# Folding a short routing tile and scoring cached keys on VectorE and POOL in a hybrid decoder step

## Chip, cores and metric

One Trainium2 chip, one of its cores. The metric is the device time of one execution in microseconds. The kernel before takes 4506.3 us, median of three runs (4504.82 to 4509.7).

## What is computed

One layer of a model with two kinds of heads and a retrieval of experts, for 512 prompt tokens (with 16 learned tokens ahead) and for 8 samples of 4 new tokens, whose past is cached: 256 keys each, in two pages of 128, found through a page table. Everything is float32. Cut to what matters here:

```python
# 8 gated-delta heads ("gdn") and 8 softmax heads with a forget gate ("fox"), head width 128
fq_s, fk_s, fv_s, logf_s = fox_inputs(qkv_fs, f_fs, ...)           # samples: 32 queries in all
k_past = cache_k[l][page_table].reshape(8, 256, FOX_HEADS, HEAD_DIM)
s = einsum('bqhd,bkhd->bhqk', q, k) * HEAD_DIM ** -0.5 + cq - ck   # each sample against its own 256 keys
p = softmax(where(kpos <= qpos, s, -inf))                         # over past and new keys
# experts: per token 8 heads, top 16 of 128 x 128 product keys, then
y = sum over 16 * 8 experts of gate * gelu(x . expert_u[idx]) * expert_v[idx]
```

## The kernel before, in words

**Groups.** 560 tokens are cut in two groups. FIRST has 256 columns (two tiles of 128; the first 32 are the samples' new tokens). LATER has 304 (tiles of 128, 128 and 48 rows). `front` (L245) runs for each: norm and gates, `heads` (L589), `mix_out`, `ffn_norm`, `route` (L2154). While LATER is worked on, a stream of expert rows runs beside it, and `rest_of_experts` finishes it.

**Heads.** In one loop of 8 heads come the projections (64 segments of 16 matmuls, L861), a gdn head and a fox head, half a head apart. Each engine has an in-order list, and it is written out by hand: every step is yielded with a mark, and `Marks` (L545) merges the lists of `gdn`, `fox`, `projections` and the like by it. 100 marks are one head; `fox_mark(h)` (L580) is 100 h + 50, called `at`. A late result therefore holds up all that stands behind it on its engine.

**The samples' cached scores.** `cached` (L767) loads 16 pages of keys and of values a head, keys on partitions. `sampled` (L1022) turns the keys on PE (L1033, 16 transposes, marks at+9 and at+12.5) into two PSUM banks; ACT (L1300) and VectorE, called DVE (L1567), copy them back. At at+17 PE adds the forget sums (L1045 to L1049) and the products of keys and queries (L1051): one 128x128 weight load for 4 columns, 16 times. DVE copies the scores (L1571), PE turns them (L1062), then softmax (L1574, L1304), turning (L1067, L1068) and values (L1076), and L1082. The prompt's own attention (L1129 to L1152) begins at mark at+`START`, which is 40, in steps of `EACH`, 24.

**What stands beside it.** At these marks gdn inverts a matrix in six levels: PE's L952 and L958 and DVE's L1479, L1483 and L1487 in turn. Then PE's L976, DVE's vN (L1500), PE's L985, ACT's copy, DVE's um (L1505) and POOL's ub (L1658), PE's L991. On SP: keys and values to scratch (L817, L822), weight loads (L747), cached pages (L776). On ACT's queue each weight segment is stored to scratch (L1199). POOL stores keys and values (L1676).

**Stream.** Each of 1088 items is an indirect load of 128 rows of 8 KB by POOL (L1854) into a ring of six, and one pass of DVE (L1932 with u, L1943 or L1947 with v). 448 items come from FIRST's routing; the rest are known when LATER's routing is done. `OVERLAP` (L306) says how many items each stage takes in: 14, 330, 48, 8 and 48, in all 448. `Share` spreads them over a stage's steps. `spread` (L1824) moves the indices of split tiles.

**Routing.** Per head PE projects queries (L2224), ACT copies them (L2245), PE scores each tile (L2232), ACT copies (L2254), DVE finds the best 16 twice: MAX8 (L2291), FIND_INDEX8 (L2294), MATCH_REPLACE8 (L2298), one each per tile and half, first on the scores, then on 80 candidates; then one-hot products over all tiles (L2342, L2345, L2347).

Of the kernel before, what the change touches and what calls it, by code (L numbers as in the profile page):

```python
# [29 lines left out]
P = 128  # L30
D = 2048
KT = D // P
# [29 lines left out]
class Group:  # L62
# [7 lines left out]

    def __init__(self, tag, base, edges, slot):
# [6 lines left out]
        self.own = slice(slot, slot + self.n)  # L78

# [111 lines left out]
def build(nc, ins, outs):  # L191
    with ExitStack() as ctx:
# [5 lines left out]
        def cst(name, a=0, b=None):  # L198
# [11 lines left out]
            "kT": nc.dram_tensor("kT_scratch", (HEADS, P, KA), F32, kind="Internal").ap(),  # L210
            "v": nc.dram_tensor("v_scratch", (HEADS, KA, HD), F32, kind="Internal").ap(),
# [94 lines left out]
OVERLAP = {"norm": 14, "heads": 330, "out": 48, "ffn": 8, "route": 48}  # L306
# [282 lines left out]
def heads(nc, ins, outs, mem, scr, group, stream, quota):  # L589
# [12 lines left out]
    PAGE_SETS = 4  # L602
# [17 lines left out]
        + ("past_turned past_even past_odd columns_ready past_scores scores_copied new_scores "  # L620
# [19 lines left out]
                "kc": ([P, PAGES, HD],), "vc": ([P, PAGES, HD],),  # L640
# [25 lines left out]
    START, EACH = (40.0, 48.0 / T) if samples else (22.0, 64.0 / T)  # L666
# [39 lines left out]
    def blocks_of(t):  # L706

        return blocks[:group.slot + t + 1]

# [23 lines left out]
    with ctx:  # L733
# [3 lines left out]
        def _(sp):  # L737
# [28 lines left out]
            def cached():  # L766
# [3 lines left out]
                for h in range(HEADS):  # L770
                    for own, buffer, used, step in (("k", B.kc, "past_scores", 36.0), ("v", B.vc, "s_out", 44.0)):
# [32 lines left out]
            def fox():  # L804
                yield -90.0
                sp.wait_ge(sem["f_cleared"], 5)
                for h in range(HEADS):
# [5 lines left out]
                    if samples:  # L813
# [6 lines left out]
                        for j in range(T):  # L820
                            a, b = blocks[j]
                            sp.dma_start(scr["v"][h, a:b, :], values_of(j)).then_inc(sem["v_kept"], 16)  # L822
                    else:
# [23 lines left out]
        def _(pe):  # L847
# [172 lines left out]
            def sampled(h, at):  # L1020
                n, q0 = h + 1, B.f_qkvT[:, h % 2, 0, :]
                yield at + 9  # L1022
                for i in range(PAGE_SETS):
                    if i == 2:
                        yield at + 12.5
                    if i == 0:
                        pe.wait_ge(sem["k_past"], n * 16 * PAGES)
                    if i < 2:
                        pe.wait_ge(sem[("f_k_copied", "f_v_copied")[i]], n)
                    else:  # L1030
                        pe.wait_ge(sem[("past_even", "past_odd")[i % 2]], h * 2 + 1)
                    for j in range(4):
                        last = nc.tensor.transpose((B.F1, B.F2)[i % 2][:, j * P:(j + 1) * P], B.kc[:, 4 * i + j, :], ident)  # L1033
                    last.then_inc(sem["past_turned"], 1)

# [1384 lines left out]
```

## Time and profile before

| | |
|---|---|
| median of three runs | 4506.3 us (4504.82 to 4509.7) |
| the profiled execution | 4511.9 us, its span 4510.2 us |
| mean granted TensorE clock | 0.753 |
| busy: PE, DVE, ACT, POOL | 53%, 74%, 13%, 52% |
| DMA | 1513.71 MB, mean 336 GB/s |

PE is TensorE's matmul part, PEld its weight loads. The shares are means over stages with different limits, so they say little: heads of FIRST run to about 890 us, LATER's front from about 1250 to 2867, the rest of the stream to the end. Times in the rows are us from the span's start; PEclk is the granted TensorE clock as a share of 2.4 GHz.

### The profile page before, as it was taken

Reading aid. Unit: us, or ns where it says so; the run is one execution under the profiler, and the core shown is the slowest. Engines: PE = TensorE matmul, PEld = TensorE weight load, DVE = VectorE, ACT = ScalarE, POOL = GpSimd, SP = SyncE. Lnnn points to the kernel's source line nnn. Section 1 sums busy time; section 2 is a strip of 40 time slices with the busy share of each in tenths; the row PEclk is TensorE's granted clock in tenths of the full one; section 3 lists DMA queues with packets and bytes.
Section 4 is the critical chain, followed back from the end, with each engine's and each line's share of the span. In section 5 each row is a group of like instructions: output and inputs, shape, how many; then the busy total and the mean of one; then the engine's idle time right before and its main releaser. Section 6 shows DMA issues by size and latency. Waiting matters only on the chain. (4 is left out here: it accounts for less than half of the span.)

```text
span 4510.2 us, 35350 instructions
## 1 busy us (share of the span) xinstructions
PE 2386.0 (53%) x11713; PEld 1883.7 (42%) x11713; DVE 3326.5 (74%) x4469; ACT 589.8 (13%) x1450; POOL 2331.3 (52%) x1217
## 2 busy tenths in 40 slices
PE   6999999898488888888849755100000000000000
PEld 5888888787466666656537544000000000000000
DVE  2333332306779999989876789899998989999997
ACT  1222222201122222222210011000000000000000
POOL 1010010000246666555665322588888888888886
PEclk8999999899699999999969877555555555555555
DMA  6766666487779999999999865699999999999998
GB/s 177 223 206 201 192 197 202 143 299 245 282 283 400 396 391 417 409 368 398 372 389 413 342 243 202 262 422 422 420 420 407 422 413 420 422 415 419 412 410 350
DMA packets 443935, 1513.71 MB, mean 336 GB/s; under 512 B 42045, under 2 KB 276209, under 8 KB 277849
## 3 DMA queue, kind: packets, MB, share of 16 engines
q0 software_dynamic: 161840, 1158.85, 63.4%
q1 hardware_dynamic: 269240, 251.94, 17.5%
q10 hardware_dynamic: 12672, 100.67, 5.6%
q8 instruction: 93, 1.52, 0.1%
q14 instruction: 90, 0.73, 0.0%
HBM read 1384.96 MB, written 126.21 MB: 335 GB/s over the span
## 5 line engine op out<-in xcount | busy, mean ns | idle before, releaser
L1932 DVE CUSTOM_DVE_ANT_0 ex_ring<-ex_ring,ex_xi 128x2048 f32<-128x2048 f32 x544 | 1244.5, 2289 | 125.4 <-DMA ex_ring<-in_peer_u_dram,ex_idx_s 45.6
L1947 DVE SCALAR_TENSOR_TENSOR ex_y<-ex_ring,ex_wt,ex_y 128x2048 f32<-128x2048 f32 x538 | 1264.4, 2350 | 96.9 <-DMA ex_ring<-in_peer_v_dram,idx_all 52.9
L1854 POOL DMA_INDIRECT ex_ring<-in_peer_v_dram,idx_all x384 | 809.2, 2107 | 252.5 <-DVE ex_y L1947 135.6
L1854 POOL DMA_INDIRECT ex_ring<-in_peer_u_dram,idx_all x384 | 786.5, 2048 | 285.1 <-DVE ex_hid L1932 175.1
L861 PE MATMUL heads_b_pj<-xnT_b,lead 128*128 128x304 f32 x2048 | 600.5, 431 | 6.9 <-PEq L283 3.6
L1886 PE MATMUL ex_fold<-ex_y,const 128*32 128x512 f32 (+1 forms) x48 | 26.9, 727 | 1090.5 <-DVE ex_y L1947 1041.3
L1886 PEld LDWEIGHTS ex_fold<-ex_y,const 128*32 128x32 f32 (+1 forms) x48 | 6.7, 143 | 1110.2 <-DVE ex_y L1947 1042.2
L1854 POOL DMA_INDIRECT ex_ring<-in_peer_v_dram,ex_idx_s x160 | 304.0, 1900 | 273.9 <-DVE ex_y L1947 192.9
L861 PEld LDWEIGHTS heads_b_pj<-xnT_b,lead 128*128 128x128 f32 x2048 | 375.4, 196 | 117.3 <-issue 14.7
L1854 POOL DMA_INDIRECT ex_ring<-in_peer_u_dram,ex_idx_s x160 | 320.2, 2001 | 190.5 <-DVE ex_hid L1932 144.8
L861 PE MATMUL heads_a_pj<-xnT_a,heads_a_w 128*128 128x256 f32 x1216 | 315.9, 397 | 1.8 <-DMA heads_a_w<-in_w_in_dram 1.8
L861 PEld LDWEIGHTS heads_a_pj<-xnT_a,heads_a_w 128*128 128x128 f32 x1216 | 226.6, 199 | 32.5 <-issue 2.9
L1904 ACT ACTIVATE ex_act<-ex_hid 128x16 f32<-128x16 f32 x34 | 7.3, 216 | 1731.0 <-DVE ex_hid L1932 1731.0
L861 PE MATMUL heads_a_pj<-xnT_a,lead 128*128 128x256 f32 x832 | 214.2, 397 | 3.5 <-PEq L281 3.5
L1850 POOL DMA_DIRECT2D ex_xi<-xi_scratch x13 | 7.0, 550 | 355.6 <-POOLq L281 300.5
L861 PEld LDWEIGHTS heads_a_pj<-xnT_a,lead 128*128 128x128 f32 x832 | 156.0, 199 | 24.7 <-issue 5.8
L2030 PE MATMUL out_b_acc<-out_b_w,mixT_b 128*128 128x256 f32 (+1 forms) x672 | 147.5, 380 | 3.3 <-DMA out_b_w<-w_out_scratch 2.6
L2030 PEld LDWEIGHTS out_b_acc<-out_b_w,mixT_b 128*128 128x128 f32 (+1 forms) x672 | 111.5, 168 | 39.3 <-issue 4.4
L1676 POOL DMA_DIRECT2D out_k_prompt_dram<-heads_a_f_kN x16 | 8.9, 561 | 220.8 <-ACT heads_a_f_kN L1295 220.8
L1658 POOL TENSOR_TENSOR heads_a_ub<-heads_a_uN,const 128x1024 f32<-128x1024 f32 x8 | 15.7, 1966 | 192.8 <-ACT heads_a_uN L1252 192.8
L2030 PE MATMUL out_a_acc<-out_a_w,mixT_a 128*128 128x256 f32 x448 | 100.5, 388 | 6.0 <-DMA out_a_w<-in_w_out_dram 6.0
L1664 POOL DMA_DIRECT2D out_gdn_sample_dram<-heads_a_sout x8 | 7.6, 952 | 181.1 <-DVE heads_a_sout L1524 181.1
(582 smaller groups left out, 4012.0 us busy)
## 6 DMA issues: line engine op xcount, KB each, us to landing
lead<-w_scratch SPq DMA_DIRECT2D x64, 1024.0 KB
heads_a_w<-in_w_in_dram SPq DMA_DIRECT2D x38, 1024.0 KB, 6.1
w_scratch<-heads_a_w ACTq DMA_DIRECT2D x38, 1024.0 KB, 4.1
lead<-in_w_in_dram SPq DMA_DIRECT2D x26, 1024.0 KB, 5.8
w_scratch<-lead ACTq DMA_DIRECT2D x26, 1024.0 KB, 4.2
out_a_w<-in_w_out_dram SPq DMA_DIRECT2D x7, 2048.0 KB, 14.0
w_out_scratch<-out_a_w ACTq DMA_DIRECT2D x7, 2048.0 KB, 7.7
out_b_w<-w_out_scratch SPq DMA_DIRECT2D x7, 2048.0 KB, 12.7
```

The source lines that it names most:

```text
L861: last = nc.tensor.matmul(pj[j % PJ][:, 0:N], slot(j)[:, k, :], xnT[:, k, :], start=(k == 0), stop=(k == KT - 1))
L1658: nc.gpsimd.tensor_tensor(B.ub[:], B.uN[:, 0, :].unsqueeze(1).to_broadcast([P, NB, HD]), cst("members", 0, NB).unsqueeze(2).to_broadcast([ ...
L1664: pool.dma_start(outs["gdn_sample"][0, :, h].rearrange("b k v -> k b v"), B.sout[:]).then_inc(sem["gs_out"], 16)
L1676: pool.dma_start(out[place, h, :], rows[own_rows, t, :]).then_inc(sem[f"{own}_out{t}"], 16)
L1850: pool.dma_start(self.tokens(s)[part.on, :], self.xi_rows[part.xi_rows]).then_inc(self.sem["xi_in"], 16)
L1854: pool.indirect_dma_start(self.ring[:, i % RING, :], None, self.tables[which], bass.IndirectOffsetOnAxis(ap=self.index(s, g, k), axis=0)). ...
L1886: last = self.nc.tensor.matmul(self.fold[0:rows, c:c + BANK], self.mem["cst"]("ident", r * rows, (r + 1) * rows), self.sum_of(s)[:, c:c + ...
L1904: self.nc.scalar.activation(self.act[:, g % 2, :], self.hid[:, g % 2, :], ACT.Gelu).then_inc(self.sem["activated"], 1)
L1932: nc.vector.tensor_tensor_reduce(ring, ring, self.tokens(s)[:], 1.0, 0.0, ALU.mult, ALU.add, self.hid[:, g % 2, k:k + 1]).then_inc(self.se ...
L1947: nc.vector.scalar_tensor_tensor(y, ring, wt, y, ALU.mult, ALU.add).then_inc(self.sem["consumed"], 1)
L2030: last = nc.tensor.matmul(acc[0:b - a, i, 0:GW], mixT[:, k, a:b], weights[:, k, :], start=(k == 0), stop=(k == KT - 1))
```

## The change

Two parts. **Routing of LATER** is folded: `folded` is true where the last tile has at most 64 rows (48 here). ACT puts the 48 query columns of an even head in the first, of an odd head in the second half of `q_fold`; even heads route two tiles, odd heads two and one of 96 rows, which holds both heads. `spread` takes the indices from there (two transfers in place of one for such a part). `OVERLAP` for routing falls from 48 to 36, so that 12 known items are left for the end.

**The cached scores** are formed from unturned keys. PE turns the 32 queries as well (behind L1104), ACT copies them to `q_row`, SP stores them to scratch (16 KB) and loads them back to all 128 partitions (`q_all`, 2 MB). For each of 8 samples a product of 2 pages x 4 queries x 128 is formed, 4 on POOL and 4 on DVE, and DVE reduces all 8 over the width. It adds the sums to PE's forget sums. Later steps of `sampled` move back by 12 marks, START and EACH become 52 and 19.

The diff below goes through OVERLAP and the helpers, then SP (cached pages, then `fox`), PE (`sampled`, then `fox`), ACT, DVE, POOL and routing.

```diff
-OVERLAP = {"norm": 14, "heads": 330, "out": 48, "ffn": 8, "route": 48}
+OVERLAP = {"norm": 14, "heads": 330, "out": 48, "ffn": 8, "route": 36}
-    START, EACH = (40.0, 48.0 / T) if samples else (22.0, 64.0 / T)
+    START, EACH = (52.0, 38.0 / T) if samples else (22.0, 64.0 / T)
+    SPLIT = NB // 2
+    def products(b):
+        shape = [P, 2, NQ, HD]
+        return (B.kc[:, 2 * b:2 * b + 2, :].unsqueeze(2).to_broadcast(shape),
+                B.q_all[:, NQ * b:NQ * (b + 1), :].unsqueeze(1).to_broadcast(shape))
...
-                                sp.wait_ge(sem[used], h)
+                                    sp.wait_ge(sem["pool_products"], SPLIT * h)
+                                    sp.wait_ge(sem["vector_products"], (NB - SPLIT) * h)
...
+                        yield at + 9.5
+                        sp.wait_ge(sem["q_rows"], n)
+                        sp.dma_start(scr["q"][h].rearrange("(q d) -> q d", d=HD), B.q_row[:]).then_inc(sem["q_kept"], 16)
+                        yield at + 12
+                        sp.wait_ge(sem["q_kept"], 16 * n)
+                        sp.dma_start(B.q_all[:].rearrange("p q d -> p (q d)"), scr["q"][h].partition_broadcast(P)
+                                     ).then_inc(sem["q_wide"], 16)
...
-                    for b in range(NB):
-                        last = nc.tensor.matmul(B.F1[:, page * NS + NQ * b:page * NS + NQ * (b + 1)], B.kc[:, 2 * b + page, :],
-                                                q0[:, NQ * b:NQ * (b + 1)], start=False, stop=(b == NB - 1))
-                yield at + 20.5
+                yield at + 32.5
-                yield at + 26
+                yield at + 38
-                yield at + 30
+                yield at + 42
-                yield at + 35
+                yield at + 47
...
+                        pe.wait_ge(sem["f_q_normed"], n)
+                        last = nc.tensor.transpose(B.F1[0:NS, 3 * P:3 * P + HD], qkv[:, 0, 0:NS], ident)
...
-                            nc.scalar.copy(B.kc[:, 4 * i:4 * i + 4, :].rearrange("p n c -> p (n c)"), B.F1[:]
-                                           ).then_inc(sem["past_even"], 1)
+                        nc.scalar.copy(B.q_row[:], B.F1[0:NS, 3 * P:3 * P + HD]).then_inc(sem["q_rows"], 1)
...
+                        for i in range(SPLIT):
+                            b = NB - SPLIT + i
+                            yield at + 16 + 3.5 * i
+                            if i == 0:
+                                dve.wait_ge(sem["q_wide"], 16 * n)
+                                dve.wait_ge(sem["k_past"], n * 16 * PAGES)
+                            nc.vector.tensor_tensor(B.product[:, 2], *products(i), ALU.mult).then_inc(sem["vector_products"], 1)
+                            yield at + 17 + 3.5 * i
+                            nc.vector.tensor_reduce(B.sK[:, :, NQ * i:NQ * (i + 1)], B.product[:, 2], AX_X, ALU.add
+                                                    ).then_inc(sem["summed"], 1)
+                            yield at + 19 + 3.5 * i
+                            dve.wait_ge(sem["pool_products"], SPLIT * h + i + 1)
+                            nc.vector.tensor_reduce(B.sK[:, :, NQ * b:NQ * (b + 1)], B.product[:, i % 2], AX_X, ALU.add
+                                                    ).then_inc(sem["summed"], 1)
+                        yield at + 31
+                        nc.vector.tensor_tensor(B.sT[:], B.F1[:, 0:2 * NS], B.sK[:].rearrange("p n q -> p (n q)"), ALU.add
+                                                ).then_inc(sem["scores_copied"], 1)
...
+                    for i in range(SPLIT):
+                        yield at + 16 + 3.5 * i
+                        if i == 0:
+                            pool.wait_ge(sem["q_wide"], 16 * n)
+                            pool.wait_ge(sem["k_past"], n * 16 * PAGES)
+                        if SPLIT * h + i >= 2:
+                            pool.wait_ge(sem["summed"], 2 * (SPLIT * h + i - 1))
+                        nc.gpsimd.tensor_tensor(B.product[:, i % 2], *products(NB - SPLIT + i), ALU.mult
+                                                ).then_inc(sem["pool_products"], 1)
...
+    def tiles_of(h):
+        rows = list(group.rows)
+        if folded:
+            rows = rows[:-1] + ([2 * fold_rows] if h % 2 else [])
+        return rows
...
+                    if folded:
+                        nc.scalar.copy(B.q[:, s, 0:fold_at], pq[s][:, 0:fold_at])
+                        place = slice(h % 2 * fold_rows, (h % 2 + 1) * fold_rows)
+                        last = nc.scalar.copy(B.q_fold[:, s, place], pq[s][:, fold_at:N])
```

ACT's and DVE's marks of the samples' softmax move back by 12 like PE's. In routing every operation of ACT and DVE goes over `tiles_of(h)` and the first T tiles of its buffers.

## Rows read from the trace of the kernel before

**Rows 1.** Stretches: PE, PEld, DVE, ACT, POOL busy; PEclk; DMA share; GB/s
```profile
128.90:841.10 712.20, 697.23 (x3978) 607.17 (x3978) 227.77 (x688) 190.56 (x463) 69.73 (x77) 0.95 0.64 198
2708.70:2744.60 35.90, 21.33 (x76) 15.19 (x76) 32.83 (x99) 3.43 (x20) 9.91 (x6) 0.79 0.64 233
2880.00:4480.00 1600.00, 16.66 (x32) 4.31 (x30) 1470.32 (x973) 9.30 (x23) 1372.78 (x643) 0.51 1.01 417
```

**Rows 2.** One line, L1104: ns least/median/most, first and last start
```profile
L1104 PE MATMUL heads_a_F<-const,heads_a_f_qkvT x16: 272/273/273, 129.1 to 841.2; 128*128 128x128 f32 x16
```

**Rows 3.** Groups by shape, DVE, one route head (2708.7 to 2744.6)
```profile
L2291 DVE MAX8 route_b_top<-route_b_sc 128x8 f32<-128x128 f32 x8 | 1.7, 280 | 0.1
...
L2342 DVE TENSOR_TENSOR route_b_hot<-route_b_place,const 128x816 f32<-128x816 f32 x1 | 1.0, 1008 | 0.0
...
L2342 DVE TENSOR_TENSOR route_b_hot<-route_b_place,const 128x768 f32<-128x768 f32 x1 | 1.0, 959 | 0.0
...
L2291 DVE MAX8 route_b_top<-route_b_sc 48x8 f32<-48x128 f32 x4 | 0.9, 268 | 0.0
```

**Rows 4.** Timeline, DVE, the same head (start, us, what)
```profile
2725.89 1.24 DVE L2291 MAX8 route_b_top<-route_b_sc 128x8 f32<-128x128 f32 x6
...
2727.35 0.28 DVE L2294 FIND_INDEX8 route_b_at<-route_b_top,route_b_sc 128x8 uint32<-128x128 f32 x1
...
2727.61 0.29 DVE L2294 FIND_INDEX8 route_b_at<-route_b_top,route_b_sc 128x8 uint32<-128x128 f32 x1
```

**Rows 5.** Timeline, seam of routing and rest, and DVE's last items
```profile
2862.57 4.82 DVE L1947 SCALAR_TENSOR_TENSOR ex_y<-ex_ring,ex_wt,ex_y 128x2048 f32<-128x2048 f32 x2 [0.58 <-DVEq L170]
...
2866.59 1.67 POOL L1854 DMA_INDIRECT ex_ring<-in_peer_u_dram,idx_all  x1 [0.30 <-issue]
...
2875.16 2.29 DVE L1932 CUSTOM_DVE_ANT_0 ex_ring<-ex_ring,ex_xi 128x2048 f32<-128x2048 f32 x1 [7.77 <-DMA ex_ring<-in_peer_u_dram,idx_all]
...
4488.30 4.81 DVE L1947 SCALAR_TENSOR_TENSOR ex_y<-ex_ring,ex_wt,ex_y 128x2048 f32<-128x2048 f32 x2
```

**Rows 6.** Groups by shape, PE, heads of the first group (128.9 to 841.1)
```profile
L1051 PE MATMUL heads_a_F<-heads_a_f_qkvT,heads_a_kc 128*128 128x4 f32 x224 | 33.6, 282 | 0.0
...
L1033 PE MATMUL heads_a_F<-const,heads_a_kc 128*128 128x128 f32 x112 | 14.5, 273 | 0.0
```

**Rows 7.** Stretches of 4 us behind L1051 (columns as rows 1)
```profile
446.00:450.00 4.00, 4.00 (x33) 3.98 (x32) 0.00 (x0) 0.00 (x0) 0.00 (x0) 0.86 0.77 229
450.00:454.00 4.00, 4.00 (x15) 3.23 (x15) 0.23 (x1) 0.00 (x0) 0.00 (x0) 0.50 0.00 0
```

**Rows 8.** Timeline, PE, head 3 (start, us, what)
```profile
434.98 0.38 PE L1104 MATMUL heads_a_F<-const,heads_a_f_qkvT 128*128 128x128 f32 x2
...
450.44 3.78 PE L861 MATMUL heads_a_pj<-xnT_a,heads_a_w 128*128 128x256 f32 x8
454.01 1.06 PE L952 MATMUL heads_a_R<-heads_a_yX,heads_a_EN 128*128 128x128 f32 x4
...
464.08 0.38 PE L985 MATMUL heads_a_R<-heads_a_vN,heads_a_yX 128*128 128x128 f32 x2
```

**Rows 9.** DMA landings of L822 (v_scratch), then of w_out_scratch
```profile
DMA to landing us min/median/max: 1.6/3.4/6.4
...
DMA to landing us min/median/max: 6.2/7.7/12.2
```

**Rows 10.** One line each: ns least/median/most, first and last start
```profile
L1524 DVE TENSOR_TENSOR heads_a_sout<-heads_a_sout,heads_a_R x8: 1220/1222/1222, 182.6 to 880.2; 128x1024 f32<-128x1024 f32 x8
...
L1644 POOL TENSOR_TENSOR heads_a_sout<-heads_a_state,heads_a_tails x8: 1887/1997/2032, 90.7 to 801.9; 128x1024 f32<-128x1024 f32 x8
...
L1505 DVE TENSOR_SCALAR heads_a_um<-heads_a_uN,const x8: 285/288/2024, 158.9 to 863.4; 128x128 f32<-128x128 f32 x8
```

**Rows 11.** Timeline, last head: PE and POOL
```profile
862.58 0.30 PEld L985 LDWEIGHTS heads_a_R<-heads_a_vN,heads_a_yX 128*128 128x128 f32 x2 [0.92 <-DVE heads_a_vN L1500]
...
863.46 1.89 POOL L1658 TENSOR_TENSOR heads_a_ub<-heads_a_uN,const 128x1024 f32<-128x1024 f32 x1 [17.73 <-ACT heads_a_uN L1252]
```

More of the change, by code:

```diff
@@ L78, in __init__ @@
         self.own = slice(slot, slot + self.n)
+        self.folded = self.n > 1 and 2 * self.rows[-1] <= P
     def prompt_rows(self, i):
@@ L770, in cached @@
                 for h in range(HEADS):
-                    for own, buffer, used, step in (("k", B.kc, "past_scores", 36.0), ("v", B.vc, "s_out", 44.0)):
+                    for own, buffer, step in (("k", B.kc, 36.0), ("v", B.vc, 46.0)):
                         for i in range(PAGES):
@@ L1021, in sampled @@
                 n, q0 = h + 1, B.f_qkvT[:, h % 2, 0, :]
[L1022 to L1034, printed above, removed]
                 yield at + 17
-                pe.wait_ge(sem["past_even"], 2 * n)
-                pe.wait_ge(sem["past_odd"], 2 * n)
+                pe.wait_ge(sem["f_k_copied"], n)
+                pe.wait_ge(sem["f_v_copied"], n)
+                pe.wait_ge(sem["q_rows"], n)
                 pe.wait_ge(sem["columns_ready"], n)
@@ L1700, in __init__ @@
             self.on = slice(p, p + rows.stop - rows.start)
+            self.folded = group.rows[tile] if group.folded and tile == group.n - 1 else 0
             first = group.base + group.tiles[tile][0]
@@ L1827, in spread @@
                 for table, source in ((self.idx_s, self.mem["idx_all"]), (self.gate_s, self.mem["gate_all"])):
-                    sp.dma_start(table[part.on, s.at:s.at + s.groups * TOPK],
-                                 source[part.rows, part.slot, part.head:part.head + s.groups, :].rearrange("p h k -> p (h k)")
-                                 ).then_inc(self.sem["spread"], 16)
+                    place = table[part.on, s.at:s.at + s.groups * TOPK]
+                    if part.folded:
+                        place = place.rearrange("p (h e k) -> p h e k", e=2, k=TOPK)
+                        for e in range(2):
+                            rows = slice(part.rows.start + e * part.folded, part.rows.stop + e * part.folded)
+                            sp.dma_start(place[:, :, e, :], source[rows, part.slot, part.head + 1:part.head + s.groups:2, :]
+                                         ).then_inc(self.sem["spread"], 16)
+                    else:
+                        sp.dma_start(place, source[part.rows, part.slot, part.head:part.head + s.groups, :]
+                                     .rearrange("p h k -> p (h k)")).then_inc(self.sem["spread"], 16)
     def spread_all(self, group):
-        return sum(32 * len(s.parts) for s in self.sets if not s.whole and (s.group is FIRST or s.group is group))
+        return sum(64 if part.folded else 32 for s in self.sets if not s.whole and (s.group is FIRST or s.group is group)
+                   for part in s.parts)
     def gather(self, pool, taken):
@@ L2252, in _ @@
                         act.wait_ge(sem["scores_read"], h)
[L2253 removed]
+                    for i, r in enumerate(tiles_of(h)):
                         last = nc.scalar.copy(B.sc[0:r, i, s, :], ps[s][0:r, i * KEYS:(i + 1) * KEYS])
@@ L2302, in _ @@
                 order = Counter(dve, sem["dve_order"], h, 100)
+                rows = [slice(0, r) for r in tiles_of(h)]
+                T = len(rows)
+                own = slice(group.slot, group.slot + T)
                 share.take(dve, h * PARTS + 1)
@@ L2305, in _ @@
                     dve.wait_ge(sem[f"scores_copied{s}"], h + 1)
-                rows = [slice(0, r) for r in group.rows]
                 top16(order, [(B.sc[rows[t], t, s, :], B.top[rows[t], t, s, :], B.at[rows[t], t, s, :])
```

113 lines of the change are left out of this document (61 added, 52 removed).

## Prediction

> **What bounds the kernel now.** I read the table of stretches first, then groups, timelines and landings. Three stretches matter. In the first group's heads (L1104 starts once a head, from 129.1 to 841.2: seven periods of 101.7 us [rows 2]) PE is busy 697.2 of 712.2 us, DVE 32% and DMA 0.64: PE sets the time, and sits idle only 2 us a head [rows 1]. Routing of the later group (one head period, 2708.7 to 2744.6) has DVE busy 32.8 of 35.9 us with DMA at 0.64: DVE sets it. From 2880 on DMA stands at 1.01: the expert stream is bound by transfers [rows 1]. So a change pays in heads if it leaves PE less to do without making PE wait; in routing if it shortens DVE.
>
> **Folded routing.** Even heads of the later group drop the 48-row tile; odd heads take it for both, 96 rows in one, and an instruction's time does not depend on its rows: MAX8 takes 268 ns on 48 rows and 280 on 128 [rows 3]. In the timeline six MAX8 take 1.24 us (0.21 each) and finds follow at 0.26 to 0.27 [rows 4], as I take for replaces. A tile dropped is 2 x (2 x 0.21 + 2 x 0.27 + 0.27) = 2.4 us on scores, about 1.0 on candidates (the 80-wide forms), and a third of six instructions over 816 and 768 elements, (1008 - 959) / 48 = 1.02 ns an element: 3 x (0.28 + 0.26) = 1.6; smaller ones 0.3. That is 5.3 us, and four even heads make **-21.2 us**. DVE hides nothing of it. ACT's and PE's chain to the next scores runs under DVE's items and table work, and keeps cover with 1.1 items a step in place of 1.5; if not, DVE waits, which is a rival below.
>
> Twelve stream items move behind routing: 12 x 2.42 us off DVE (L1947, 2.35 and a gap) = -29.0, and back at the stream's pace. That pace is (4493.1 - 2875.2) / 640 items = 2.53 us [rows 5]: +30.3. But the seam changes. Now all 448 known items are used up in routing; the first gather with new indices is issued at 2866.6 and DVE sits until 2875.2, 7.8 us [rows 5]. Afterwards six landed items wait in the ring. DVE's last route item ends at 2867.3 - 21.2 - 29.0 = 2817.1; a barrier, 1 us by choice; the next gather follows its first item (2.4) and lands 8.6 later (the same 2866.6 to 2875.2): 2829.1; then 646 items x 2.528 = 1633.1, end 4462.2 against 4493.1. **Folding in all: -31 us**, bounds -24 (the seam gives nothing) and -33. The four more small index transfers are needed hundreds of us later: nothing.
>
> **Cached scores, what PE loses.** 16 transposes a head go (L1033, 14.5 us in seven heads, 1.76 in place, where neighbours overlap), and 32 passes of four columns (L1051, 33.6 / 7 = 4.8 us) [rows 6]. Behind L1051 the granted clock falls, to 0.86 and then 0.50, which is the 1.2 GHz level [rows 7], and the eight L861 at 450.4 take 3.57 us to the next row [rows 8], in place of 1.73 where the clock is full. From L1104 (434.98) to L985 (464.08), 29.1 us [rows 8], PE would be done in 19.6: removed 1.76 + 4.45, clock 1.84 + 0.8, L1062, L1067 and L1068 moved behind (1.2), one added transpose and its wait (0.5). Alone this would be -8.4 us a head.
>
> **What it gets instead** is a chain from L1104 to L985. ACT copies keys, then queries: 1.1 us. SP is behind its two L822 issues: q write issued at +1.5. Landing: least / median / most of L822's v_scratch stores are 1.6 / 3.4 / 6.4 us [rows 9]; I take 3.4, since it stands in the same queue. The broadcast (2 MB into 128 partitions) has no row; the nearest with its bytes and 16 KB runs is w_out_scratch, 6.2 / 7.7 / 12.2 [rows 9]; I take 7.7, the median, as other transfers run beside both. So queries are wide at **+12.7 us**, bounds +9.4 and +15 (a quarter of both slow sides). Estimate from the Trainium skill (DMA: Bandwidth & Descriptors, Bandwidth and the anatomy of one DMA), which gives about 436 GB/s and 2 us fixed: 6.8 us, by which the sum would end 7 us lower; no row here shows a broadcast undisturbed.
>
> From there DVE, in order: before the vN that L985 waits for stand four multiplies and seven reductions of 1024 elements. L1524 of that size takes 1.22 us [rows 10], 1.25 with the gap to the next: 13.8 us. Four of gdn's own (0.42) and vN (0.34) make 15.8. POOL's products (L1644's shape, 2.0 us) read two SBUF operands meanwhile, and DVE's L1505, 0.29 us by its median, took up to 2.02, beside POOL's L1658 [rows 10, 11]: the two exclude each other. Laid out with DVE first wherever both come free together, one multiply waits 0.6 us and hops add 0.3: **16.7 us**. So L985 starts at +12.7 + 16.7 = +29.4 in place of +29.1: the whole PE gain is waited away, **+0.3 a head**. Two smaller terms: PE, idle 40% of 16 us there, loses clock as in [rows 7], of which most is hidden under DVE: +1.0, between 0 and 2.6 (all of it shown). And um (L1505) now comes behind a reduction, so after POOL's ub: 1.5 us later, of which 0.5 is not covered by five L861. Together 1.8 x 7 = **+12.6 us**, without a price for SP's wait (3.5 us; weights are loaded four segments ahead), nor for POOL, whose products end before ub is due; key and value loads wait for products long done. Scores of the prompt, moved from 40 to 52, displace 0.65 us of DVE work into the busy convolution and take as much out: nothing.
>
> The **last head** has no fillers. L1104 to L985 takes 21.4 us now (841.2 to 862.6 [rows 2, 11]) and would take 29.2: +7.8; L1076 (5.2) leaves the path to L991 but returns before L999, and the prompt's scores, 3 us of PE, with their maximum and exponential fall behind L1017, where now they are done before it. **+10.7 us**, between +7 and +17.
>
> Sum against the profiled execution (4511.9): -31 + 12.6 + 10.7 = **-7.7, 4504.2**. It stands 5.6 us above the median of 4506.3, so about **4498**. About 0.2% (9 us) is what a measurement of this kernel tells from no change.
>
> **Rivals.** *Queries arrive early* (the least landings of both [rows 9]): at +9.4, L985 at +26.1, -3 a head, with the other terms -1.9 x 7 - and tail +7.4: 4511.9 - 31 - 13 + 7 - 5.6 = 4469. For it: DMA is at 0.64 on the mean of the stretch [rows 1]; against: w_scratch stores of 1 MB stand beside it. *POOL takes the port first* (ends on the other side): on each of three ties between the products of one batch DVE waits 2.0 us more, L985 at +35.4, (6.3 + 1.5) x 7 = 55, tail +16.7: 4547. It decides once more than one tie a head is lost (4514 at one). L1505 mostly won its tie (median 288 ns of eight [rows 10]); for two-operand products nothing shows it. The Trainium skill (SBUF — State Buffer, Who interferes with whom) says that whoever issues first has the shared pair for the whole instruction and that reductions never contend; L1505's 2.02 us agrees with the first, who wins a tie no row tells. *Late landing or clock*: +2.3 a head and +2 in the tail, 4516. *Folding hits ACT's or PE's chain*: about -12 in place of -31: 4517. *DVE's work is hidden* and PE keeps its gain: -59, no tail: 4416; against it: 29.4 us of chain in a 19.6 us gap.
>
> **Chances.** Forecast (4485 to 4512) 0.32; early 0.25; POOL 0.18; late or clock 0.16; folding 0.05; hidden 0.04. Faster than 4497.3: early, hidden and 0.13 of the forecast, 0.42; within 0.2%: 0.18 of the forecast and 0.07 of late and folding, 0.25; slower 0.33. The range takes in early and most of POOL: 4460 to 4541; the forecast's own is 4485 to 4512.
>
> **What would show it.** Route heads at 27 (even) and 32.3 us (odd); no 7.8 us gap at the seam. In heads: PE busy falls by 5 to 10 us a head but the period stays 101 to 104 us, PE waits at L952's and L958's lines for DVE, DVE waits for q_wide's DMA some 6 us a head, L1104 to L985 near 29 us. Wrong if the period falls under 98 us, if DVE multiplies show 3 us means (POOL first), or if landings differ from 7.7.

## The result, and the profile after

The changed kernel takes **4533.0 us**, median of five runs (4530.0 to 4538.4), against 4508.9 of five runs of the kernel before: ratio 1.005, 95% interval 1.0039 to 1.0061. It is slower by 0.5%. Forecast were 4498 us, a little faster than before, so the sign is the other one; the range (4460 to 4541) holds 4533. All medians leave out the slow executions, one of e7 (5816.7 us) and one of the kernel before (5396.6). The profiled execution took 4532.8, its span 4531.1.

From both traces, start of each part in us of the span (the first key turning, L1104 before and L1112 now; the first matmul of `mix_out`; of the later group's heads; the first MAX8 and the last `gate_all` of its routing; the end of the last item):

| | before | after | added by the part |
|---|---|---|---|
| first key turning | 129.1 | 127.5 | -1.6 |
| last key turning, seven periods on | 841.1 | 872.5 | **+33.0** (101.7 to 106.4 a head) |
| `mix_out` of FIRST | 892.9 | 940.8 | **+16.5** (last head, 51.8 to 68.3) |
| LATER's heads | 1255.0 | 1307.2 | +4.3 |
| LATER's routing | 2577.7 | 2626.1 | -3.8 |
| its last `gate_all` | 2861.8 | 2861.6 | **-48.6** |
| end of the stream | 4493.1 | 4514.0 | +21.1 |

Folding gives 27.5 us, as the last two rows say (-48.6 and +21.1), and the cached scores cost 48, the sum of the others. The table of stretches of the kernel after, for seven head periods, for PE's wait in head 3 and what follows it, and for the rest of the stream (columns as [rows 1]):

```profile
127.46:872.47 745.01, 668.28 (x3648) 564.08 (x3647) 321.97 (x758) 183.99 (x455) 155.03 (x105) 0.95 0.66 210
...
461.50:468.00 6.50, 0.24 (x2) 0.00 (x0) 2.65 (x3) 0.00 (x0) 2.63 (x1) 0.87 0.85 292
468.00:472.00 4.00, 3.82 (x11) 3.28 (x12) 3.53 (x4) 0.00 (x0) 4.00 (x3) 0.50 0.01 4
...
2880.00:4480.00 1600.00, 25.27 (x48) 6.35 (x48) 1472.01 (x975) 9.31 (x23) 1366.38 (x644) 0.51 1.01 418
```

Against [rows 1] PE has less to do (3648 matmuls in seven periods in place of 3978, 95.5 us busy a head in place of 99.6), but it now stands still for 745.0 - 668.3 = 76.7 us, 11.0 a head; before it was 2.1. What it waits for, from the waits of PE in these heads (us in total, times, longest):

```profile
PE heads_a_R L976 <- DVE heads_a_yX L1492: 49.9, 7, 11.1
PE heads_a_R L1000 <- DVE heads_a_yX L1492: 10.7, 7, 1.5
```

L976 and L1492 are the inversion's steps that were L952 and L1483. The timeline of DVE in head 3, whose keys are turned at 450.13:

```profile
455.12 0.42 DVE L1488 TENSOR_TENSOR heads_a_yX<-heads_a_R,const 128x256 f32<-128x256 f32 x1 [2.71 <-PE heads_a_R L976]
465.32 1.23 DVE L1581 TENSOR_TENSOR heads_a_product<-heads_a_kc,heads_a_q_all 128x1024 f32<-128x1024 f32 x1 [9.77 <-DMA heads_a_q_all<-q_scratch]
466.58 1.22 DVE L1584 TENSOR_REDUCE heads_a_sK<-heads_a_product 128x8 f32<-128x1024 f32 x1
467.72 0.41 DVE L1492 TENSOR_TENSOR heads_a_yX<-heads_a_yX,heads_a_R 128x256 f32<-128x256 f32 x1
...
468.89 1.22 DVE L1588 TENSOR_REDUCE heads_a_sK<-heads_a_product 128x8 f32<-128x1024 f32 x1 [0.44 <-POOL heads_a_product L1708]
470.15 2.00 DVE L1581 TENSOR_TENSOR heads_a_product<-heads_a_kc,heads_a_q_all 128x1024 f32<-128x1024 f32 x1
```

DVE stands 9.8 us before its first product (10.3 on the mean of eight heads; some 6 were forecast), with the inversion's L1492 listed behind it. On PE, where eight L861 (now L885) end at 461.7, the answer is one line, and the vN matmul (L985, now L1009) comes 31.5 us behind the keys in place of 29.1 [rows 8]:

```profile
468.18 1.22 PE L976 MATMUL heads_a_R<-heads_a_yX,heads_a_EN 128*128 128x128 f32 x4 [6.45 <-DVE heads_a_yX L1492]
...
481.64 0.49 PE L1009 MATMUL heads_a_R<-heads_a_vN,heads_a_yX 128*128 128x128 f32 x2
```

The landings of the queries' store (L839), then of the broadcast (L845):

```profile
DMA to landing us min/median/max: 2.9/3.6/6.7
```

```profile
DMA to landing us min/median/max: 7.4/9.3/10.3
```

The times of single lines: DVE's multiply, POOL's product, DVE's um (L1505 before, [rows 10]):

```profile
L1581 DVE TENSOR_TENSOR heads_a_product<-heads_a_kc,heads_a_q_all x32: 1224/1226/2009, 147.3 to 900.5; 128x1024 f32<-128x1024 f32 x32
```

```profile
L1708 POOL TENSOR_TENSOR heads_a_product<-heads_a_kc,heads_a_q_all x32: 2335/3361/3390, 147.4 to 896.6; 128x1024 f32<-128x1024 f32 x32
```

```profile
L1514 DVE TENSOR_SCALAR heads_a_um<-heads_a_uN,const x8: 1528/1529/1530, 165.0 to 904.9; 128x128 f32<-128x128 f32 x8
```

### The profile page after: what moved, and what is told of

It reads as the page before. It is cut to its first block and busy times, and to the rows that moved or that the text cites. A ratio compares the mean times of both kernels' runs of the same rounds, so it can differ in the third digit from the quotient of the medians.

```text
span 4531.1 us, 34650 instructions
## 1 busy us (share of the span) xinstructions
PE 2339.7 (52%) x11321; PEld 1832.3 (40%) x11321; DVE 3414.0 (75%) x4453; ACT 580.9 (13%) x1442; POOL 2414.5 (53%) x1249
## 5 line engine op out<-in xcount | busy, mean ns | idle before, releaser
L1988 DVE SCALAR_TENSOR_TENSOR ex_y<-ex_ring,ex_wt,ex_y 128x2048 f32<-128x2048 f32 x538 | 1264.7, 2351 | 97.4 <-DMA ex_ring<-in_peer_v_dram,idx_all 52.2
L885 PE MATMUL heads_b_pj<-xnT_b,lead 128*128 128x304 f32 x2048 | 600.4, 431 | 7.4 <-PEq L286 3.6
L885 PEld LDWEIGHTS heads_b_pj<-xnT_b,lead 128*128 128x128 f32 x2048 | 374.6, 195 | 118.3 <-issue 14.3
L885 PE MATMUL heads_a_pj<-xnT_a,heads_a_w 128*128 128x256 f32 x1216 | 314.3, 396 | 1.9 <-DMA heads_a_w<-in_w_in_dram 1.9
L885 PEld LDWEIGHTS heads_a_pj<-xnT_a,heads_a_w 128*128 128x128 f32 x1216 | 225.9, 199 | 31.3 <-issue 2.3
L885 PE MATMUL heads_a_pj<-xnT_a,lead 128*128 128x256 f32 x832 | 215.6, 398 | 3.5 <-PEq L284 3.5
L885 PEld LDWEIGHTS heads_a_pj<-xnT_a,lead 128*128 128x128 f32 x832 | 156.3, 200 | 24.2 <-issue 5.3
L1708 POOL TENSOR_TENSOR heads_a_product<-heads_a_kc,heads_a_q_all 128x1024 f32<-128x1024 f32 x32 | 99.0, 3113 | 92.8 <-DMA heads_a_q_all<-q_scratch 88.2
L1581 DVE TENSOR_TENSOR heads_a_product<-heads_a_kc,heads_a_q_all 128x1024 f32<-128x1024 f32 x32 | 45.4, 1419 | 83.1 <-DMA heads_a_q_all<-q_scratch 82.2
## 6 DMA issues: line engine op xcount, KB each, us to landing
out_a_w<-in_w_out_dram SPq DMA_DIRECT2D x7, 2048.0 KB, 14.2
```

The costliest lines, as they stand in the source:

```text
L885: last = nc.tensor.matmul(pj[j % PJ][:, 0:N], slot(j)[:, k, :], xnT[:, k, :], start=(k == 0), stop=(k == KT - 1))
L1581: nc.vector.tensor_tensor(B.product[:, 2], *products(i), ALU.mult).then_inc(sem["vector_products"], 1)
L1708: nc.gpsimd.tensor_tensor(B.product[:, i % 2], *products(NB - SPLIT + i), ALU.mult).then_inc(sem["pool_products"], 1)
L1988: nc.vector.scalar_tensor_tensor(y, ring, wt, y, ALU.mult, ALU.add).then_inc(self.sem["consumed"], 1)
```

## The experiments

Each was timed in three rounds beside the kernel before; ratios are to that. "Start" is DVE's first product and "vN" the first vN matmul, both in us behind the keys' turning and as a mean of seven heads; period, idle time of PE and its busy time are per head over the same seven; the last column is the last head, from its keys' turning to `mix_out`.

| kernel | ratio, 95% interval | start | vN | period | PE idle, busy | last |
|---|---|---|---|---|---|---|
| before | 1 | | 28.9 | 101.7 | 2.1, 99.6 | 51.8 |
| after | 1.0050, 1.0039 to 1.0061 | 15.9 | 32.2 | 106.4 | 11.0, 95.5 | 68.3 |
| e1 fold only | 0.9940, 0.9924 to 0.9957 | | 28.9 | 101.7 | 2.1, 99.6 | 51.7 |
| e2 scores only | 1.0106, 1.0089 to 1.0123 | 15.7 | 32.0 | 106.7 | 11.1, 95.6 | 66.7 |
| e3 early data | 0.9905, 0.9888 to 0.9921 | 5.7 | 24.5 | 98.5 | 5.7, 92.8 | 59.9 |
| e4 6 marks later | 1.0062, 1.0039 to 1.0084 | 15.6 | 28.5 | 108.3 | 11.3, 97.1 | 63.6 |
| **e5 wide marks** | **0.9871**, 0.9854 to 0.9889 | 18.9 | 20.0 | 95.1 | 2.2, 92.9 | 64.7 |
| e6 POOL once | 1.0038, 1.0027 to 1.0049 | 16.2 | 31.6 | 104.9 | 10.7, 94.2 | 67.3 |
| e7 ACT's store | 1.0055, 1.0033 to 1.0077 | 15.3 | 31.6 | 106.3 | 10.6, 95.8 | 67.7 |
| e8 halves | 1.0036, 1.0021 to 1.0051 | 12.4 | 31.3 | 105.2 | 9.4, 95.8 | 67.7 |
| e9 PE, wide marks | 0.9983, 0.9974 to 0.9993 | | 20.1 | 102.6 | 1.2, 101.4 | 60.2 |
| e10 narrow pitch | 0.9978, 0.9968 to 0.9987 | 18.7 | 20.0 | 102.3 | 4.8, 97.4 | 66.7 |
| e11 START only | 1.0049, 1.0032 to 1.0066 | 15.8 | 32.1 | 106.1 | 10.7, 95.4 | 68.4 |
| e12 fold, 48 items | 0.9964, 0.9953 to 0.9975 | | | | | |
| e13 um first | 0.9879, 0.9862 to 0.9895 | 18.7 | 20.0 | 95.3 | 3.1, 92.2 | 64.2 |
| e14 twice, after | 1.0203, 1.0186 to 1.0220 | 24.3 | 40.6 | 115.8 | 19.7, 96.1 | 78.9 |
| e15 twice, wide | 1.0061, 1.0044 to 1.0077 | 26.0 | 20.0 | 105.4 | 10.0, 95.4 | 74.3 |

**Which half.** e1 is the kernel before with the folding and its 36 items, e2 with the cached scores.

> The folded routing and its 36 items alone, on the kernel before; the cached scores stay on PE. In the changed kernel's trace the stretch from the first MAX8 of the later group's routing to the last route item is 48.9 us shorter than before and the rest of the stream 21.4 us longer. Theory (the parts add): -27.5 us, 4481.5 against 4509. Rival (the fold's gain depends on what the other part does to the stream ahead of routing, which also moved by +0.5 us): less than -20 or more than -35. First group's heads unchanged, period 101.7.

> The cached scores' new way alone, on the kernel before; routing unfolded with 48 items. Theory (the parts add): +48 us, 4557 against 4509, made of -1.6 before the first head, +33 in seven heads (period 106.5), +16.5 in the last head and +4.3 up to the later group, less 4 in its heads. Rival (a part of the +52 up to the later group is given back behind it, where DVE and the stream bind and not PE): less than +35.

e1 took 4484.0 (before: 4509.9), e2 4560.1. In e1's trace the span is 30.8 us shorter. So the parts add: -26 and +50 of the medians, +24 measured. The slower result is the scores' alone.

**Late queries, or work.** e3 fills `q_all` from the input, sooner, so the sample scores are formed from other numbers:

```diff
+                        yield at - 4
...
+                        sp.dma_start(B.q_all[:].rearrange("p q d -> p (q d)"),
+                                     ins["x_prompt"][0, 0:2].rearrange("a b -> (a b)").partition_broadcast(P)
+                                     ).then_inc(sem["q_wide"], 16)
...
-                        sp.dma_start(B.q_all[:].rearrange("p q d -> p (q d)"), scr["q"][h].partition_broadcast(P)
-                                     ).then_inc(sem["q_wide"], 16)
```

> Changed kernel, but all partitions are filled with 16 KB of the prompt's input instead of the queries, 13 marks sooner, so that the same 2 MB have landed before the products; the queries' store to scratch and SP's wait for it stay. The sample scores are so formed from other numbers. Theory (late queries: DVE stands some 10 us a head in its list, with the inversion's steps behind it, and PE follows): no wait for q_wide, PE idle in the heads under 3 us each, period 97 to 99 instead of 106.5, and the last head 5 to 9 us shorter: 4460 to 4475. Rival (what costs is DVE's own 20 us of products and sums, and the port shared with POOL, wherever they lie): period 103 or more, 4510 or more.

4470.8: the same DVE and POOL work costs 62 us less, and the period falls below the one before. PE's idle time, 5.7, is more than the 3 expected. Part of the reason, PE's wait of 1.7 us a head for an inversion step behind DVE's first multiply, shows in POOL's and DVE's timelines, where this time POOL starts first:

```profile
427.92 4.65 POOL L1710 TENSOR_TENSOR heads_a_product<-heads_a_kc,heads_a_q_all 128x1024 f32<-128x1024 f32 x2
```

```profile
428.52 5.15 DVE L1583 TENSOR_TENSOR heads_a_product<-heads_a_kc,heads_a_q_all 128x1024 f32<-128x1024 f32 x1
433.70 1.22 DVE L1586 TENSOR_REDUCE heads_a_sK<-heads_a_product 128x8 f32<-128x1024 f32 x1
```

POOL's two products run to 432.57, and DVE's multiply ends 1.1 us behind them: it waited for both, and so in seven of eight heads. This is the rival "POOL takes the port first", and it is real, only not what decides here.

**Price of POOL.** e6 lets POOL form two products in the first head and none later (half of the samples' scores are then left as they were), DVE's list is the same:

```diff
-                            dve.wait_ge(sem["pool_products"], SPLIT * h + i + 1)
+                            dve.wait_ge(sem["pool_products"], i % 2 + 1)
...
-                    for i in range(SPLIT):
+                    for i in range(2 if h == 0 else 0):
```

> Changed kernel in which POOL forms two products in the first head and none later, and DVE sums up those old ones: half of the samples' scores are wrong from then on, and DVE's own work and its list are unchanged. It prices the shared port and the waits for POOL's products. Theory (late queries are most of the loss): the 2.00 us multiply falls to 1.23 and a 0.4 us wait goes, q_wide stays at +15 us, period 1.0 to 1.5 us shorter, last head 1 to 3: 4520 to 4527. Rival (POOL's hold of the port slows more than the multiply): 3 us a head or more, below 4512.

It took 4528.8 (before: 4511.7), 1.8 above the range expected; behind the first head every multiply takes 1.23 us, and the period is 1.5 shorter. So by the trace the shared port and the waits for POOL's products cost 11 us in seven heads; by the medians the whole run gains only about 5 (ratio 1.0038 in place of 1.0050), and the profiled execution (4516.3) was the fastest of eight. The rival, 3 us a head or more, fell.

**Sooner queries.** e7 has ACT copy the queries first and store them from its own queue. e8 does the same, cuts the broadcast in two (DVE's samples first) and puts two of DVE's own products at the head of its list.

```diff
+                        act.wait_ge(sem["q_rows"], n)
+                        act.dma_start(scr["q"][h].rearrange("(q d) -> q d", d=HD), B.q_row[:]).then_inc(sem["q_kept"], 16)
```

```diff
+                        for e, name in enumerate(("q_wide", "q_wide2")):
+                            sp.dma_start(B.q_all[:, e * half:(e + 1) * half, :].rearrange("p q d -> p (q d)"),
+                                         scr["q"][h, e * half * HD:(e + 1) * half * HD].partition_broadcast(P)
+                                         ).then_inc(sem[name], 16)
```

> Changed kernel, but ACT copies the queries before the keys and issues their store from its own queue at once, so that they don't stand behind SP's four stores of keys and values; SP keeps the broadcast. Theory (each us by which the queries land sooner is a us off L1112 to the vN matmul and off the period): store issued at +1.2 in place of +2.7 us, q_wide at +13 in place of +15.9, period 2 to 3 us shorter, 4510 to 4520. Rival (the broadcast's landing takes up what the store gains, since it meets the same stores of 1 MB): q_wide less than 1 us sooner, 4527 or more.

> As the one with ACT's store, and the broadcast is cut in two of 1 MB, DVE's four samples first, POOL's behind; DVE's list begins with two of its own products, POOL's sums come later. DVE's and POOL's work is the same. Theory (late queries): DVE's first product at +9.5 to +11 us, vN matmul at +27 to +28.5, period 101 to 103, last head 3 us shorter: 4490 to 4505. Rival (a landing is mostly latency, or both halves share the engines and land together): first product at +12.5 or later, 4510 or more.

Both missed. e7 (4535.1) goes with its rival: the broadcast's landing rose from 9.3 to 10.1 us by the median, and the start moved 0.6 us. e8 (4525.0) starts 3.5 us sooner, at +12.4, which is short of the +9.5 to +11 expected, and the vN matmul comes only 0.9 us sooner: it still waits for all the sums, and POOL's half of the queries lands at +14.2 to +17.2 in the seven heads, only 0.6 us sooner on the mean than the whole did. What the two show is that landing sooner is hard here; that it would pay, even in this order, e3 has shown.

**The order of DVE's list.** e4 moves all from the products on 6 marks back; e5 moves the products to +29 in steps of 4.5, behind the inversion and the first vN, and what follows 17 marks back:

```diff
-    START, EACH = (52.0, 38.0 / T) if samples else (22.0, 64.0 / T)
+    START, EACH = (67.0, 24.0 / T) if samples else (22.0, 64.0 / T)
...
-                            yield at + 16 + 3.5 * i
+                            yield at + 29 + 4.5 * i
...
-                        yield at + 31
+                        yield at + 48
```

> Changed kernel with every step from the products to the samples' last one 6 marks later (products at +22, scores added at +37), the prompt's attention at 58 in place of 52 (steps of 16 in place of 19), cached pages 6 marks later. The queries land as late as before, but DVE has the inversion's steps ahead of the wait. Theory (it is the order in DVE's list that turns a late landing into PE's idle time): DVE waits under 3 us a head, period 97 to 100, last head the same or up to 6 us longer: 4470 to 4495. Rival (the chain of products and sums is too long wherever it begins, so PE waits for it and for the vN step behind it): period 104 or more, 4520 to 4545.

> Changed kernel with the products behind the gated-delta head's first vN step: at +29 in steps of 4.5 marks (before +16, 3.5), all later sample steps 17 marks later, prompt's attention at 67 in steps of 12. With 6 marks of delay PE still waited 6.1 us for the inversion's last level (L1492) and 3.8 us for um (L1514), both listed behind a product. Theory (PE's idle time is that of gdn steps listed behind products or their wait): L1492 comes first, one wait for um of at most 3 us stays, PE idle 2 to 4 us a head, period 98 to 101, last head 5 us longer: 4485 to 4510. Rival (20 us of work on DVE need room, and later they meet the next head's convolution): period 104 or more, 4525 or more.

e4 took 4540.5, a miss: its rival's number. DVE waited only 2.7 us for queries in head 4, yet the timeline of PE there has two waits:

```profile
585.09 3.62 PE L1000 MATMUL heads_a_R<-heads_a_state,heads_a_apart 128*32 128x128 f32 x16 [6.09 <-DVE heads_a_yX L1492]
597.47 0.76 PE L1015 MATMUL heads_a_R<-heads_a_um,heads_a_kN 128*128 128x128 f32 x2 [3.84 <-DVE heads_a_um L1514]
```

The last level's L1492 and then um stood behind products. With L1492 ahead of all products and um ahead of the second, e5 takes **4454.3** us against 4511.7 before, 1.3% faster, and 79 us less than the changed kernel. Period and time are both under what was expected (98 to 101, and 4485 to 4510). The queries land no sooner (10.1 us median for the broadcast). Its seven periods:

```profile
128.53:794.57 666.04, 650.35 (x3648) 557.11 (x3647) 326.96 (x758) 183.98 (x455) 148.84 (x105) 0.97 0.74 234
```

**Controls.** e9 is the fold alone with the cached scores on PE, but the samples' steps and the prompt's attention as late as in e5 (turning 17 marks later, softmax and values 29). e11 is the changed kernel with only START and EACH of e5.

> Control for the wide marks: folded routing, cached scores on PE as before, but the samples' steps moved as far back as in the version with wide marks (turning 17 marks later, softmax and values 29, prompt's attention at 67 in steps of 12). Theory (the wide marks help only because DVE's products no longer stand ahead of gdn's steps; where PE never waits, a later place changes nothing): period 101 to 102.5, same as the fold alone, 4484 within 10 us, last head 0 to 10 longer. Rival (a later place of softmax, values and attention is worth something by itself, as in clock or convolution): period under 99, 4470 or less.

> Changed kernel with the prompt's attention alone at 67 in steps of 12, products and all sample steps where the change put them. Theory: PE's wait for the last levels (6.4 and 1.5 us a head) is untouched, period 105 to 107, 4533 within 8 us. Rival (the attention's place made the gain of the wide marks): 4515 or less.

e9 (4502.8 against 4509.2) has the period expected within 0.1 us, but missed in time: it was to be within 10 us of e1 and is 19 slower, by 0.9 us a head, 8.4 in the last head and a few behind. A later place by itself gains nothing. e11 took 4530.4, as expected. So the gain of e5 is PE's relief from cached scores, with the products out of the inversion's way.

**One step out of place.** e10 is e5 with the products in steps of 3.5 marks. e13 is e10 with the second and later products 0.7 mark later.

```diff
-                            yield at + 29 + 3.5 * i
+                            yield at + 29 + 3.5 * i + 0.7 * (i > 0)
```

> The version with wide marks, but the products in steps of 3.5 marks as in the changed kernel, in place of 4.5; everything else as there (products from +29 on). Theory (their place behind the last level and vN is what counts): period 95 to 97, 4454 within 8 us. Rival (it was the wider spacing that let the head's steps between): PE idle over 5 us a head, 4475 or more.

> The version with steps of 3.5 marks, whose period stayed at 102.4 (PE waits 3.6 us for um, L1514, listed behind the second product), with the second product and what follows put 0.7 mark later, so that um stands ahead of it; nothing else moves. Theory (one gdn step behind a product costs its own wait and then the halved clock that follows it): PE waits under 1 us for um, granted clock 0.96 or more in seven heads, period 95 to 97, 4454 within 8 us. Rival (four products in 14 marks are too dense wherever um stands): period 99 or more.

e10 missed: 4501.9, a period of 102.3. Its timelines of DVE and PE, then two stretches of 4 us around:

```profile
556.90 1.48 DVE L1581 TENSOR_TENSOR heads_a_product<-heads_a_kc,heads_a_q_all 128x1024 f32<-128x1024 f32 x1
558.31 2.36 DVE L1514 TENSOR_SCALAR heads_a_um<-heads_a_uN,const 128x128 f32<-128x128 f32 x1
```

```profile
560.81 0.76 PE L1015 MATMUL heads_a_R<-heads_a_um,heads_a_kN 128*128 128x128 f32 x2 [3.62 <-DVE heads_a_um L1514]
```

```profile
557.00:560.80 3.80, 0.19 (x1) 0.02 (x1) 3.80 (x3) 0.00 (x0) 3.80 (x3) 0.89 0.87 226
560.80:565.00 4.20, 4.19 (x19) 3.48 (x20) 4.13 (x5) 0.00 (x0) 3.90 (x2) 0.50 0.15 45
565.00:569.00 4.00, 4.00 (x12) 2.85 (x11) 0.62 (x1) 0.00 (x0) 1.58 (x1) 0.50 0.31 86
```

At 33 marks um comes due; the second product at 32.5 is ahead of it, and um itself runs beside POOL's product (2.36 us). PE stands 3.6 us and then works at the 1.2 GHz level for 8 us. e13, with the product at 33.2, takes 4454.0 (before: 4512.0): um in 0.60 us, 3.1 us idle, granted clock 0.98 in place of 0.92. In head 4 the traces list the same instructions in the same order on all engines but for um, which DVE has one place earlier. That one place is worth 48 us here, 7 us a head, of which the idle time is 1.7 and PE's slower work 5.2.

**Doubling the lateness.** e14 and e15 are the changed kernel and e5 with the broadcast issued a second time when the first has landed.

```diff
+                                     ).then_inc(sem["q_first"], 16)
+                        yield at + 21
+                        sp.wait_ge(sem["q_first"], 16 * n)
+                        sp.dma_start(B.q_all[:].rearrange("p q d -> p (q d)"), scr["q"][h].partition_broadcast(P)
                                      ).then_inc(sem["q_wide"], 16)
```

> Changed kernel that broadcasts the queries twice, one after the other: nothing is computed otherwise, and they are ready 8 to 10 us later, at +24 to +26. Theory (with the last levels listed behind the products each us of lateness is a us of the period or more, by the clock): period 114 to 118, last head 7 to 9 longer: 4600 to 4640. Rival (the wait is partly covered by fillers on PE): period under 110, below 4575.

> The version with wide marks that broadcasts the queries twice. There the products begin at +18.65 and queries were ready by about +15, so 3.5 us of lateness are hidden and the rest falls on DVE with um, S and the second vN listed behind. Theory: q_wide at +24 to +26, 6 us of wait, PE idle 6 to 8 us, period 102 to 106: 4510 to 4550, less harm than the same doubling does to the changed kernel. Rival (behind vN lateness costs nothing): period under 98.

e14 took 4603.2: the products start 8.4 us later and a head is 9.4 longer, 1.1 us for each; the last head is 10.6 longer, where 7 to 9 were expected. Its longest wait of PE in head 4, the 6.43 us of the changed kernel grown by the lateness:

```profile
618.82 1.22 PE L980 MATMUL heads_a_R<-heads_a_yX,heads_a_EN 128*128 128x128 f32 x4 [14.89 <-DVE heads_a_yX L1496]
```

e15 took 4536.9, in its range, but the expectation that it would suffer less than e14 fell: products start 7.1 us later, the period is 10.2 longer, and doubling costs 83 us there against 70. Wide marks hide some 3 us of lateness (broadcast issued at 5.5, landed 10.1 later, wanted at 18.7) and nothing after: PE then waits for um, listed behind the first product, 62.7 us in seven heads.

**Folding and the seam.** e12 is e1 with 48 items in routing.

> Folded routing on the kernel before with 48 items in routing, not 36: all known items are used up in it as before. Theory (folding itself takes 21 us off DVE, and the 12 items left give back the seam of 7.8 us): routing 29 us longer than with 36, no items at its end, DVE idle 7 to 8 us at the seam, 8 to 11 us behind the fold with 36: 4492 to 4495. Rival (the seam's idle time is filled or hidden anyway): the same as with 36, 4484.

It took 4491.3, 7 us behind e1 (4484.0), a little less than the 8 to 11 expected. From the first MAX8 to the last `gate_all` routing takes 265.8 us, against 284.1 unfolded and 235.3 in e1. The timelines of DVE at the seam, e12 and then the kernel after:

```profile
2850.68 2.29 DVE L1943 CUSTOM_DVE_ANT_0 ex_ring<-ex_ring,ex_xi 128x2048 f32<-128x2048 f32 x1 [7.15 <-DMA ex_ring<-in_peer_u_dram,idx_all]
```

```profile
2862.09 4.82 DVE L1988 SCALAR_TENSOR_TENSOR ex_y<-ex_ring,ex_wt,ex_y 128x2048 f32<-128x2048 f32 x2 [0.23 <-DVEq L172]
2868.46 12.18 DVE L1988 SCALAR_TENSOR_TENSOR ex_y<-ex_ring,ex_wt,ex_y 128x2048 f32<-128x2048 f32 x5 [1.55 <-PEq L286]
```

## Why the prediction was wrong

**Folding: right.** Forecast -31, found -27.5 in the changed kernel, -30.8 in e1's span and -26 in its medians (interval -34 to -19). Routing became 48.6 us shorter (48.8 in e1) against the 50.2 summed (21.2 and 29.0): an even head saves 4.9 us (35.9 to 31.0 in e12) where 5.3 were summed. The seam's gap fell from 7.8 to 1.6 us, and e12 shows that only the items left over do that. Route heads take 28.2, 34.2 and 28.4 us (even) and 30.6 to 31.5 (odd) where 27 and 32.3 were forecast.

**Heads: the step that failed is the time at which queries are wide.** Forecast +12.7, bounds +9.4 and +15; measured 14.3 to 15.9 in six heads and 19.9 in the first, 15.9 on the mean. Three terms of the sum were too small; on the mean of the seven heads (where the views above have medians of eight) they are these. The store is issued at +2.8, not +1.5, and in the first head at +5.7. SP has four stores of keys and values ahead of it, which in head 3 are issued by +2.6, where before they were by +1.4: issuing the two of keys took 1.97 us in place of 0.82, and why is not shown. It lands in 4.1, not 3.4. The broadcast lands in 8.9, not 7.7. In the first head, where the DMA share was 0.78 while it ran, it landed in 7.4; in head 3, with a store and a load of weights, 1 MB each, beside it, the share was 1.01 and it landed in 9.7 (columns as [rows 1]):

```profile
139.90:147.40 7.50, 0.00 (x0) 0.00 (x0) 0.06 (x1) 0.00 (x0) 0.01 (x1) 0.64 0.78 316
455.66:465.30 9.64, 6.08 (x41) 5.20 (x40) 0.00 (x0) 0.00 (x0) 0.00 (x0) 1.00 1.01 374
```

How much of the landing is due to what runs beside it no run separates. The estimate from the Trainium skill (DMA: Bandwidth & Descriptors, Bandwidth and the anatomy of one DMA), 6.8 us, was 2.5 short of the median; it is near the least landing of any run, 6.9 in e11. The Trainium skill gives it for transfers that GpSimd issues, and these go by SP. The rest of the chain held: from queries to the vN matmul 16.3 us in the seven heads against 16.7. So that matmul is at +32.2 in place of +29.4, and 3.3 us later than before in place of 0.3. The other terms, 1.5 forecast, are 1.4 (4.7 - 3.3). Three us in seven heads are 21, less 0.7 for the other terms: the heads' sum is 20.4 short, 33.0 against 12.6. e14 agrees with the slope, 1.1 us of period for each us of lateness.

**Last head.** +16.5 against +10.7: the vN matmul came at 31.1 in place of 21.5, +9.6 against 7.8, and the chain behind it took 6.9 more, where 2.9 were summed; which step of it was longer no run separates. Another 4.3 us between the first group's heads and the later group's were not forecast, and stay open; e2, without the folding, has 3.2 of them.

**The whole sum.** From profiled execution to profiled execution -7.7 were forecast and +20.9 measured. Of these 28.6 the seven heads are 20.4, the last head 5.8, folding 3.5, and the three stretches without a forecast together -1.1. The other 6 us up to 4533 are mostly the 5.6 taken off in the forecast to come from the profiled execution to the median: after the change the profiled execution (4532.8) is at the median.

**The rivals.** "Late landing or clock" had the right mechanism (chance 0.16) and too small a price: its 2.3 us a head beyond the forecast were 2.9, its 2 us in the last head 5.8. "POOL takes the port first" did not happen in the changed kernel: DVE won the first tie, and in each head one of its four multiplies took 2.00 us, 0.8 lost where 2.0 were priced. e3 shows it: 5.15 us, 3.9 lost, twice the price of one tie. The Trainium skill (SBUF — State Buffer, Who interferes with whom) says that whoever issues first has the shared pair for the whole instruction, and this agrees, with one thing more: two of POOL's products in a row kept DVE out all the while. That reductions don't contend agrees as well: L1588 took 1.20 to 1.22 us in the changed kernel with POOL's products beside it. "DVE's work is hidden" had 0.04, against it a chain of 29.4 us in a gap of 19.6. That was right for the list as written, and e5 shows that the gap is not given: with the products behind vN, that matmul is at +20.0 and PE keeps 6.6 us a head. In "Queries arrive early" the -1.9 us a head does not follow from its terms: -3.0 and the other 1.5 make -1.5, and 4472 in place of 4469.

**What would have been decisive.** The working counted the inversion's steps into DVE's chain and foresaw PE's wait at them, but took the order of the list as given, and never priced another. The wait for queries held back the inversion's L1492, and PE with it, for 7.1 us a head (the first wait above), and PE came out of it at the halved clock. Of idle time 8.8 us a head were added, of PE's work only 4.1 were saved, since part of what went was paid back in slower matmuls: the same 3648 are busy for 92.2 us a head in e13, 95.5 in the changed kernel and 97.4 in e10.

## What to carry to other kernels

Where each engine runs an in-order list, price new work by what it stands in front of, not by its own time: find when its input arrives, and list it behind every step that another engine will want before then. If a chain to DRAM and back feeds it, take the landing from the slow side of the rows, and leave room for a late issue: the queue's other stores stand ahead. And price each new wait of TensorE twice, once for the wait and once for the slower matmuls behind it.

## What the runs showed of the hardware

- One wait of 3.6 us a head (e10) lowered the granted clock over seven heads to 0.92, from 0.98 with no wait that long (e13), and made the same matmuls 5.2 us a head slower, more than the wait itself. The price need not grow with the wait: the changed kernel, whose waits at L976 last 5.6 to 11.1 us, has a mean clock of 0.95 and matmuls 3.3 us a head slower than e13's.
- DVE's multiply of two SBUF operands waited until two POOL products in a row were done (5.15 us in place of 1.23), and POOL's product takes 3.36 us beside a DVE multiply, 2.34 at the least. um, a multiply by one column of constants, took 0.27 to 0.28 us with POOL idle (e4). It took 1.53 where POOL's ub had begun 0.4 us ahead of it (the changed kernel), 0.60 where ub had begun 1.4 ahead (e13), each time to just behind ub's end, and 2.36 beside POOL's product (e10). Before the change both began within 0.1 us of each other in every head, and um took 0.29 in six heads and 2.02 in two.
- In the changed kernel a 16 KB store to DRAM took 2.9 to 6.7 us to land (median 3.6), and the broadcast of its 16 KB to 128 partitions 7.4 to 10.3 (median 9.3). Two halves of 1 MB issued together had a median of 7.9 (e8). When the store came from another queue and sooner (e7), the broadcast's median rose to 10.1.
